# Leading panels on the un-normalised residual in a four-layer float32 decoder trunk

## The reference, cut to what matters

```python
h = layer_norm(alpha * h + half(h), g, b)      # eight times: ln1 after a mixer, ln2 after an MLP
u = (h @ w_in) * valid                         # 1024 -> 5632
y = conv_b + sum(shift(u, 2 - j) * conv_w[j] for j in range(3))
half = (silu(y[:, :2816]) * y[:, 2816:]) @ w_out
```

## Time and profile before

| what | value |
|---|---|
| median of 3 runs | 1478.29 us (1474.98 to 1480.88) |
| the profiled execution | 1474.03 us, span 1472.2 us |
| TensorE busy | 1366.9 us, 93% of the span |
| VectorE busy | 1017.4 us, 69% |
| ScalarE busy | 789.1 us, 54% |
| GpSimd busy | 447.7 us, 30% |
| granted TensorE clock, mean | 0.972 of full speed |
| weights read | 201 MB, 137 GB/s over the span |

### The profile page before, as it was taken

One profiled execution on the slowest core, in us unless ns is written; L12 is line 12 of the kernel. 1 busy time (PEld: TensorE's weight loads), 2 busy tenths in 40 slices (PEclk: granted clock), 3 DMA queues, 4 the chain that ended last, 5 costly groups with the idle time before them and its releaser, 6 DMA issues.

```text
span 1472.2 us, 30684 instructions
## 1 busy us (share of the span) xinstructions
PE 1366.9 (93%) x10501; PEld 1293.0 (88%) x10501; DVE 1017.4 (69%) x2048; ACT 789.1 (54%) x1590; POOL 447.7 (30%) x371
## 2 busy tenths in 40 slices
PE   7899899999898899999986989999997999899996
PEld 6788799999776799999965789999987888799996
DVE  4664877766786787765786767776575665877765
ACT  4554466654455466654444546665444564566643
POOL 2000544423400554333510054433350002644323
PEclk9999999999998999999998999999999999999999
DMA  7231355556321346556340134655633322366562
GB/s 266 90 112 58 115 157 185 172 185 188 121 69 40 115 137 191 171 185 188 114 130 29 58 115 131 188 179 176 192 111 112 114 87 87 106 193 186 186 213 74
DMA packets 56934, 203.38 MB, mean 138 GB/s; under 512 B 6256, under 2 KB 8336, under 8 KB 56720
## 3 DMA queue, kind: packets, MB, share of 16 engines
q1 hardware_dynamic: 56784, 202.20, 43.9%
q0 software_dynamic: 64, 0.03, 0.0%
HBM read 201.13 MB, written 1.05 MB: 137 GB/s over the span
## 4 chain that ended last, share of the span: by engine, by line
PE 78%; DVE 10%; issue 6%; ACT 4%; POOL 1%; DMA 1%; ACTq 0%; SPq 0%; DVEq 0%; POOLq 0%
PE ps L374 21%; PE ps L378 20%; PE ps L377 20%; PE ps L458 3%; PE ps L487 3%; PE ps L394 2%; PE ps L397 2%; PE ps L398 2%; PE ps L505 2%; DVE h L1125 2%; DVE w_lo L1125 2%; ACT probs L791 2%; ACT w_hi L741 1%; DVE rstd L1247 1%; DMA raw<-in_weights 1%
## 5 line engine op out<-in xcount | busy, mean ns | idle before, releaser
L1125 DVE TENSOR_TENSOR w_lo<-raw,w_hi 128x1024 fp32r<-128x1024 f32 x378 | 464.3, 1230 | 235.2 <-ACT w_hi L741 234.0
L374 PE MATMUL ps<-h_hi,w_hi 128*128 128x272 f32 (+1 forms) x1752 | 511.2, 292 | 0.9 <-DVE q_rope L1334 0.9
L377 PE MATMUL ps<-h_lo,w_hi 128*128 128x272 f32 (+1 forms) x1752 | 503.6, 287 | 0.0
L378 PE MATMUL ps<-h_hi,w_lo 128*128 128x272 f32 (+1 forms) x1752 | 503.3, 287 | 0.0
L741 ACT ACTIVATE w_hi<-raw 128x1024 fp32r<-128x1024 f32 x378 | 396.5, 1050 | 159.7 <-PE ps L374 141.4
L374 PEld LDWEIGHTS ps<-h_hi,w_hi 128*128 128x128 f32 x1752 | 331.1, 189 | 3.1 <-DVE q_rope L1334 1.2
L377 PEld LDWEIGHTS ps<-h_lo,w_hi 128*128 128x128 f32 x1752 | 331.3, 189 | 1.0
L378 PEld LDWEIGHTS ps<-h_hi,w_lo 128*128 128x128 f32 x1752 | 331.0, 189 | 0.0
L1099 POOL TENSOR_TENSOR gated<-y 128x272 f32<-128x272 f32 x88 | 133.9, 1522 | 233.7 <-DVE y L1490 233.7
L374 PE MATMUL ps<-hid_hi,w_hi 128*128 128x272 f32 (+2 forms) x644 | 189.9, 295 | 4.4 <-DVE keys L1125 1.6
L377 PE MATMUL ps<-hid_lo,w_hi 128*128 128x272 f32 (+2 forms) x644 | 185.6, 288 | 0.0
(11 more groups left out here) (155 smaller groups left out, 2134.6 us busy)
## 6 DMA issues: line engine op xcount, KB each, us to landing
raw<-in_weights SPq DMA_DIRECT2D x378, 512.0 KB, 3.6
cst<-in_consts SPq DMA_DIRECT2D x1, 1787.5 KB, 11.8
h<-in_x SPq DMA_DIRECT2D x2, 544.0 KB, 5.4
out<-h SPq DMA_DIRECT2D x8, 128.0 KB, 1.8
keys<-y POOLq DMA_DIRECT2D x2, 17.0 KB, 2.2
```

The lines of the kernel that those rows point to most:

```text
L374: m = pe.matmul(b, whi, xhi, start=n == 0, stop=False)
L377: pe.matmul(b, whi, xlo, start=False, stop=False)
L378: m = pe.matmul(b, wlo, xhi, start=False, stop=n == len(tiles) - 1)
L1125: return dve.tensor_tensor(out_, a_, b_, op)
```

## The change

Seven norms (0 to 6) are changed, with the stage that follows each.

- **x parts.** While `o` or `down` runs, ScalarE also writes `x_hi = g*h` (8 a norm) and VectorE `x_lo` (8 a norm, `x_low`, each after the join of its chunk), from the residual before normalisation; gamma and beta themselves ride along as two more columns (274 in place of 272).
- **Early panels.** The first 3 panels of `up`, `v` and `a`, and both of `vk`, are made from these parts. TensorE makes early panel 0 right behind the output stage, then the sums over partitions (`moments`), then the other early panels. The warm-up matmuls go.
- **Settling.** VectorE corrects each early panel (`settle`: four operations from PSUM into an SBUF buffer) once `rstd` is there. The consumers of these panels read the SBUF buffers.
- **Leading panels.** The next two panels (before: the first three; two for `vk`) are made as leading panels from the normalised `h`. `vk` has none, and the first `q` panel waits for `h_ready` itself.
- **Order.** The weight splits that belonged to the early panels move from the stage into the norm, on ScalarE and VectorE. On VectorE settle 0 stands behind chunk 2, the second split behind chunk 3, settle 1 behind chunk 5, the third split behind chunk 6, settle 2 behind everything.
- **GpSimd** adds chunk and square in one instruction of twice the length (6 a norm, before 12) and subtracts the mean from 5 chunks (before 3), VectorE from 3 (before 5).

```diff
-CENTER_DVE = 5
+CENTER_DVE = 3
-WARM = 40
+EARLY = {"up": 3, "v": 3, "a": 3, "vk": 2}
@@ TensorE, leading_panels
-                    for j in range(count):
+                    for j in range(start, start + count):
                         b, slot = bank(p0 + j)[:, t0:T], (u0 + j) % RING
                         if k == 0:
                             if p0 + j >= BANKS:
                                 pe.wait_ge(bank_free, p0 + j - (BANKS - 1))
                             pe.wait_ge(lo_ready, u0 + j + 1)
@@ TensorE, output
+                    for j in range(EARLY[NEXT[n]]):
+                        if j == 1:
+                            moments()
+                        panel(s, u1, p1, 0, j, lambda k: (x_hi[:, k, :], x_lo[:, k, :]), x_chunk, t0, T + 2)
@@ TensorE, stages
-                    gemm(a, "v", from_h, nr, after=after_v, lead=3 if a else 1)
+                    gemm(a, "v", from_h, nr, after=after_v, lead=2 if a else 1, straight=True)
-                    gemm(a, "vk", from_h, nr, lead=2)
-                            panel(sq, uq, pq, 0, m, from_h, None, 0)
+                            panel(sq, uq, pq, 0, m, from_h, nr, 0)
-                    gemm(a, "a", from_h, nr, after=after_a, lead=3)
+                    gemm(a, "a", from_h, nr, after=after_a, lead=2)
-                gemm(a, "up", from_h, norm_ready(2 * a + 1), lead=3)
+                gemm(a, "up", from_h, norm_ready(2 * a + 1), lead=2)
@@ ScalarE, square
                 act.activation(squares[:, k % 2, :], h[:, k, :], ACT.Square).then_inc(squared, 1)
+                if n == 2 * DEPTH - 1:
+                    return
+                if k == 0:
+                    act.activation(x_hi[:, :, T:T + 2], ln_par[:, n].rearrange("p two k -> p k two"), ACT.Copy)
+                act.activation(x_hi[:, k, 0:T], h[:, k, :], ACT.Copy,
+                               scale=ln_par[:, n, 0, k:k + 1]).then_inc(x_hi_done, 1)
@@ VectorE, gemm
-                        evac(i, j, bank(p0 + j), i * s.body + (p0 + j))
+                        evac(i, j, early_out[j] if is_early else bank(p0 + j), i * s.body + (p0 + j))
@@ VectorE, output
+                def x_low(k):
+                    ...
+                    dve.scalar_tensor_tensor(x_lo[:, k, 0:T], h[:, k, :], ln_par[:, n, 0, k:k + 1],
+                                             x_hi[:, k, 0:T].bitcast(F32), ALU.mult,
+                                             ALU.subtract).then_inc(x_ready, 1)
                 def before(i, j):
                     k = i * 4 + j
+                    if k == 2:
+                        x_low(0)
+                    if k >= 2:
+                        x_low(k - 1)
...
+                def settle(j):
+                    ...
+                    dve.wait_ge(panel_done, p1 + j + 1)
+                    copy(g_and_b[:, j, :], b[:, T:T + 2])
+                    own.link(tt(u, b[:, 0:T], rstd[:], ALU.mult))
+                    own.link(dve.scalar_tensor_tensor(u, mean_rstd, g_and_b[:, j, 0:1], u, ALU.mult, ALU.subtract))
+                    dve.tensor_scalar(u, u, -1.0, g_and_b[:, j, 1:2], ALU.mult, ALU.add).then_inc(settled, 1)
+
+                x_low(DC - 1)
+                split_early(0)
...
                 own.link(dve.reciprocal(rstd[:], rstd[:]))
+                own.link(tt(mean_rstd, mean, rstd[:], ALU.mult))
...
                     if k and not last:
                         lo_part(k - 1)
+                    if k == 2:
+                        settle(0)
+                    if k in (3, 6):
+                        split_early(k // 3)
+                    if k == 5:
+                        settle(1)
                 if not last:
                     lo_part(DC - 1)
+                    settle(2)
@@ GpSimd, norm
-                    pool.tensor_tensor(total[:], h[:, 0, :] if k == 1 else total[:], h[:, k, :],
-                                       ALU.add).then_inc(total_added, 1)
...
+                    pool.tensor_tensor(totals[:], with_square(0) if k == 1 else totals[:], with_square(k),
+                                       ALU.add).then_inc(sums_added, 1)
```

More of the change, by code:

```diff
@@ L158, with early_of @@
 LAST_FROM = {"o": N_META - 2, "up": N_META - 2, "down": N_META}
-WARM = 40
+QROW = T + 8
+EARLY = {"up": 3, "v": 3, "a": 3, "vk": 2}
+EARLY_BEFORE = [sum(EARLY[NEXT[i]] for i in range(n)) for n in range(2 * DEPTH)]
+def early_of(layer, name):
+    if name not in EARLY or (layer == 0 and name != "up"):
+        return 0, 0
+    n = 2 * layer if name == "up" else 2 * layer - 1
+    return EARLY[name], EARLY_BEFORE[n]
 ROPES = [sum({"fox": 0, "swa": 1 + 8, "mla": 1 + 4}[k] for k in KINDS[:a + 1]) for a in range(DEPTH)]
@@ L225, in c @@
             return cst[0:rows, a:b]
-        shift, total_sq, mean_sq, mean = (y[:, i, :] for i in range(4))
+        shift, mean_sq, mean = y[:, 0, :], y[:, 2, :], y[:, 3, :]
+        mean_rstd = mean_sq
+        total, total_sq = totals[:, 0, :], totals[:, 1, :]
+        early_out = (squares[:, 0, :], squares[:, 1, :], total)
         ident, ones = c("ident"), c("ones")
@@ L354, in _, with panel @@
         def _(pe):
[L355 removed]
+            def panel(s, u0, p0, i, j, rhs, ready, t0, end=T):
                 pn = i * s.body + (p0 + j)
[L358 removed]
+                b = ps[:, (p0 + j) % s.banks, t0:end]
                 if not (isinstance(pn, int) and pn < s.banks):
@@ L404, in gemm @@
                 t0 = LAST_FROM.get(name, 0) if layer == DEPTH - 1 else 0
+                early, _ = early_of(layer, name)
                 def turn(i):
                     for j in range(s.body):
[L408 to L411, removed]
+                        led = isinstance(i, int) and i * s.body + j < early + lead
+                        if not led:
                             panel(s, u0, p0, i, j, rhs, ready, t0)
+                        elif i * s.body + j == early:
+                            leading_panels(s, u0, p0, rhs, ready, early, lead, t0)
+                            for jj in range(j):
+                                if after is not None:
+                                    after(i, jj)
+                        elif i * s.body + j < early:
+                            continue
                         if after is not None:
@@ L419, in gemm @@
                 elif lead:
-                    turn(0)
-                    turns(pe, s.turns, turn, first=1)
+                    unrolled = -(-(early + lead) // s.body)
+                    for i in range(unrolled):
+                        turn(i)
+                    turns(pe, s.turns, turn, first=unrolled)
                 else:
@@ L524, in output, with moments @@
[L524 to L527, removed]
-                if n < 2 * DEPTH - 1:
[L530 to L534, removed]
+                def moments():
+                    pe.wait_ge(shift_ready, n + 1)
+                    pe.wait_ge(sums_added, 6 * (n + 1))
+                    pe.matmul(ps[:, 5, 0:T], ones, total, start=True, stop=False)
+                    pe.matmul(ps[:, 6, 0:T], ones, total_sq, start=True, stop=False)
+                    pe.wait_ge(bank_free, p0 + 8)
+                    pe.matmul(ps[:, 5, 0:T], ones, h[:, 7, :], start=False, stop=True).then_inc(mean_done, 1)
+                    pe.wait_ge(squared, 8 * n + 8)
+                    pe.matmul(ps[:, 6, 0:T], ones, squares[:, 1, :], start=False, stop=True).then_inc(sq_mean_done, 1)
@@ L758, in turn @@
                     for j in range(s.body):
-                        for u in units_of(layer, name, i, j):
-                            split_hi(u)
+                        if not (isinstance(i, int) and i == 0 and j < early):
+                            for u in units_of(layer, name, i, j):
+                                split_hi(u)
                         if evac is not None:
@@ L845, in output, with split_early @@
                 square(n, 7)
+                last = n == 2 * DEPTH - 1
+                def split_early(j):
+                    if not last and j < EARLY[NEXT[n]]:
+                        for u in units_of((n + 1) // 2, NEXT[n], 0, j):
+                            split_hi(u)
+                split_early(0)
                 act.wait_ge(mean_done, n + 1)
@@ L1141, in gemm @@
                 s, _, p0 = LAYERS[layer][name]
+                early, before_early = early_of(layer, name)
                 def turn(i):
@@ L1155, in gemm @@
                         turn(i)
+                elif early:
+                    turn(0)
+                    turns(dve, s.turns, turn, first=1)
                 else:
```

98 lines of the change are left out of this document (68 added, 30 removed).

## The result

The changed kernel takes 1556.09 us (median of 4 runs, 1552.41 to 1557.85), the kernel before 1476.63 beside it: ratio 1.053, 95% interval 1.050 to 1.056. It is slower by 79.5 us. The profiled execution took 1557.85 us, its span is 1556.1.

What follows compares the result with a forecast made beforehand. TensorE, busy 93%, bounds the kernel, but VectorE is the resource to price in the norms. Even norms 46.4, odd 19.8, clock 14: +80 us on 1474.03, so 1554; the median stands 4.3 higher: 1558 us, range 1505 to 1582.

Steps and rivals of the forecast that it cites:

- x parts in `o`: Norms 0, 2, 4, 6: VectorE's added `x_low` moves the join of chunk 7 by 3.4 us; ends 0 and 5.9.
- Sums behind early panel 0: Between last join and M (first subtraction of the mean): M comes later, +2.6 us in even norms, +3.4 in odd.
- The merged addition: GpSimd in `o`: one addition taken at 2.7 us, like the present pair, so it keeps the pace and isn't late.
- VectorE from M to the free bank: After M (first subtraction of the mean), even norms: bank free at M+21.9, fifth panel at M+27.8, before M+22.2: +5.6 us.
- The clock: TensorE's leads after standing: slow clock costs 2.0 us at each of seven norms, 14 us; ends 0 and 15.
- Odd norms: Norms before `v`, `a`, `vk`: 3.4 + 3.6 us, twice, and 3.4 + 2.4: 19.8 us together, without the clock.
- the three matmuls: Sign on TensorE: three leading matmuls, then idle, all others following at one go, the first at clock 0.50.
- The stand: Sign on TensorE: after three leading matmuls it idles some 15 us, released by VectorE's consumer of early panel 0.
- the way from M to the first step like L1490: Sign on VectorE: from M, first subtraction of the mean, to that step's end grows from 17.5 to about 22 us.
- Rival 1: Leading panels: the bank wait does not end last, they follow `h_ready`; together +12 us, 1490 us; chance 0.07.
- Rival 2: Early panels cover the norm, VectorE's settles and splits fitting its idle time; about -37 us, 1441 us; chance 0.08.
- Rival 3: Warm-up matters little and contention falls with merged additions; only odd norms and tail stay: 1518 us, no separate chance.

Runs made afterwards that it cites:

- Experiment 7: `odd` with x parts also made, but unused, in the even norms during `o`: 1504.02 us, ratio 1.019 to the kernel before.
- experiment 5: Kernel before with one edit: GpSimd adds chunk and square in one instruction of twice the length; 1490.93 us, ratio 1.009.
- experiment 4: Changed kernel with GpSimd's additions of chunk and square as two instructions again: 1554.90 us, ratio 1.0518 to the kernel before.
- fill: The filler: changed kernel with 96 unread matmuls between early and leading panels; 1543.26 us, ratio 1.0445 to the kernel before.
- warm0: Kernel before without its 40 warm-up matmuls at each norm and the wait before them: 1486.40 us, ratio 1.0057.
- settled: Changed kernel, but a panel following an early panel in its bank waits only until that panel is settled: 1520.82 us, ratio 1.029 to the kernel before.
- experiment 8: Changed kernel with the bank wait of `settled` and 40 unread matmuls between early and leading panels: 1526.73 us, ratio 1.033 to the kernel before.
- odd: `settled` plus GpSimd's additions split, early panels only behind odd norms, old order before `up`, VectorE centring 3 chunks: 1483.78 us, ratio 1.004 to the kernel before.
- center3: Kernel before with one edit: VectorE subtracts the mean from 3 chunks, GpSimd from 5; 1470.39 us, ratio 0.9946.

## Why the prediction was right

Forecast 1558, measured 1556.09. The mechanism was the forecast one: TensorE makes three leading matmuls and stands for the bank of early panel 0, late x parts and late sums come on top, and the slow clock behind. That the sum is within 2 us is luck, for its terms are off by up to 2.3 us in a norm, with both signs. By the steps of the prediction, at norm 0 unless said:

- **x parts in `o`: right in kind, too small.** From the join of chunk 1 to the end of that of chunk 7 went 16.2 us and now go 21.8: +5.7, forecast 3.4 with an upper end of 5.9. The other three `o` show the same, +5.6. Experiment 7 gives about 5 a norm. Chunk 2 comes 1.5 us late where the forecast had 0.9, each later one 0.82 where it had 0.50. `x_low` does not cost 0.50; beside GpSimd it costs 1.6, and L1321, which scales the old residual, gives 0.5 back. The rule cited from the Trainium skill (GPSIMD Engine Reference, section 1, Specifications), that GpSimd and VectorE contend when the VectorE instruction has two SBUF inputs, was the better guide than L1252, which ran beside additions of beta, with one SBUF tensor. Those additions are not free of it either: beside them L1258 takes 0.72 us, and 0.50 before they begin. By that rule the term would have been 5.9 (an estimate), near the 5.7 measured.
- **Sums behind early panel 0: right.** M came 5.71 us after the join, before 2.84: +2.9, forecast +2.6. In odd norms +2.7, forecast +3.4. These are readings of the trace; no experiment took this term out alone.
- **The merged addition:** taken as neutral on its pace. Alone it costs 14 us (experiment 5), beside `x_low` nothing (experiment 4), so the sum was not hurt. The premise was wrong and only its place made it harmless.
- **VectorE from M to the free bank: right, and too long.** Forecast M+21.9, measured 205.12, M+19.8. A settle takes 1.3 to 1.5 us and not 1.7, since the links cost 0.04 each: 0.8 us of the 2.1. Most of the rest is in the eight low parts, where rescaling takes 0.50 us for each chunk and not the up to 0.72 of before.
- **The clock: too small.** 2.8 us in this lead, forecast 2.0. The fifth panel is done at M+28.3 against a forecast of M+27.8 plus 2.0. The filler gives 12.8 us back, the forecast said 14; the warm-up alone is worth 8.2. The Trainium skill's rule (TensorE: Matmul & The Clock Gate, part 1), that the slow clock is the default and only activity lifts it, agrees with the 0.50 behind the stand of norm 0 and with `warm0`.
- **Odd norms.** The sixth panel of `a` starts at 788.32, M+28.8, before M+23.5: +5.3, forecast 3.6 and the clock 2.0. That of `v` starts at M+31.6, before M+27.1: +4.6, and from the seventh on +5.8, for transposes of the values stand behind the pair. `vk`'s first `q` panel starts at M+16.5, +0.7 for 2.4.

Per norm the errors of +2.3 and +0.8 against -2.1 nearly cancel. From join to join of the whole trace the four even norms cost 54.0 us, forecast 46.4 and the clock 8; the three odd ones 26.8, forecast 19.8 and the clock 6. So the split between the two kinds was right as well.

Of the signs of the prediction, the chunk of `o` (3.44, forecast 3.1 or more) and the three matmuls came as said. The stand is 12 us and not 15, and the way from M to the first step like L1490 grows to 19.8 and not 22.

Rival 1 (pace of the low parts) is refuted by the three matmuls and the stand. `settled` makes its condition true, with the lead done at M+18.9, and takes 1521 us where the rival said 1490: the rival was priced 31 us too low. Rival 2 (faster) is refuted too: even without the bank wait 43 us of loss are left, from x parts, late sums, settles, splits and clock together. Rival 3 (the low end) fails with the x parts at 5.7 and the filler's 13 us. Singly, the bank wait is worth 35 us and the filler 13, both taken off the changed kernel, and the x parts in `o` 20, added to `odd`; they overlap (experiment 8) and may not be added.

About 2.4 us of the profiled difference lie in the attention of layer 0, ahead of any changed norm: the first join of its `o` comes 2.5 us late, and from 60 to 62 us the granted clock is 0.77 where before it was 1.00. `center3`, whose edit comes later as well, reached that join 2.4 us late too, and `fill` did not, so it belongs to an execution, not to the change.

## What to carry to other kernels

Before moving work into a gap of one engine, write down the list of the engine that makes the gap. Here TensorE had 90 us to fill and VectorE, in the norms and in `o`, next to none to give; the corrections lengthened the gap that they should fill. And a buffer is free when its counter says so: when a result leaves its bank early, the count that the next user waits for must move with it.

## What the runs showed of the hardware

GpSimd and VectorE, with two SBUF tensors each, did not slow down in proportion; these rows look as if they took turns. GpSimd's addition of 544 columns in `o` takes 1.70 us whether VectorE's operation in its way is `x_low` (1.58) or L1224 (1.60), and that operation ends about 0.3 us after the addition; in the changed kernel the next one, L1321, takes its 0.43. With the addition in two halves two operations take 1.0 each. The join, which reads one operand from PSUM, takes 0.44 beside GpSimd's second addition before the change (171.03, beside 170.66 to 171.62) as it does alone. So one contending operation can't be priced by itself, only the chunk: 2.63, 3.12 and 3.45 us.
